# Last feed-forward, first half: activations and remainders in 512 columns, VectorE folds the pairs, ScalarE squares

## Chip, cores and metric

One Trainium2 chip, one NeuronCore. The metric is the device time in microseconds of one execution of the whole program; lower is better. All data are float32; matrix products run on values that are rounded to TensorE's fp32r format, with a correction for what the rounding drops.

## What is computed

The program is two model blocks one after the other on 256 tokens of width 1024 (`T = 256`, `DC = 8` chunks of 128 features). The change touches the last feed-forward of the second block alone:

```python
def sqrelu_mlp(h, w1, w2):
    return jnp.square(jax.nn.relu(h @ w1)) @ w2
...
        h_lat = h_lat + mod_l[5] * sqrelu_mlp(modulate(rmsnorm(h_lat, norm2_g[i]), mod_l[3], mod_l[4]),
                                              mlp_w1[i], mlp_w2[i])
    return rmsnorm(h_lat, final_g)
```

`h @ w1` widens 1024 features to 4096, which are `MC = 32` tiles of 128 features by 256 tokens; `@ w2` brings them back. Beside it run the dot products of the conditioning vector with `ada_w` (the `mod` values), of which eight tiles fall into this stage.

## The kernel before

**Split products.** A weight tile `w` is split into `whi = round(w)` (ScalarE, L930) and `wlo = w - whi` (VectorE, L1428); activations likewise into `xhi` and `xlo`. A product is the sum of three matmuls: `whi·xhi + whi·xlo + wlo·xhi`, each with 256 moving columns (one per token), into 256 columns of a PSUM bank.

**Units.** Weights stream from DRAM in units of 128 x 1024 floats (512 KB), 8 blocks of 128 x 128. In this stage (`mlp_up`, 32 units) one unit gives one output tile, so a unit is 8 blocks, 24 matmuls and one tile. The second half (`mlp_down`, 32 units) makes a tile of 4 units. It already uses the other form that `units` has (`both=m2`): rounded values and remainders lie in one buffer, a matmul of 512 columns takes `whi` against both at once, and one of 256 columns takes `wlo` against the rounded values, so a bank holds two partial results side by side.

**Rings.** There are four slots each for `raw` (as landed), `whi` and `wlo`, and four PSUM banks for tiles. SP issues the load of the next position when the slot four positions back is done with (`slots_done`, signalled by L1428 or by the dot product L1515, which takes a position of its own after every fourth unit).

**Order of work.** Every engine runs its own list of instructions strictly in the order in which the code emits it; semaphores are counters. In step j of the stage, for tile j:

- ScalarE: `hi()` rounds the weights of the unit three ahead (it waits for the load, and for TensorE to be done with unit j-1); then Relu from the PSUM bank into `mr` (L1382, waits `pe_units`, signals `tile_read`); then the rounding of tile j-1 of the squares, `mhi` (L1377, waits `y_f32`, signals `yhi_ready`).
- VectorE: the square `ms = mr*mr` (L2057, waits `tile_read`, signals `y_f32`); the remainder `mlo` of tile j-1 (`inner_lo`, L2052, waits `yhi_ready`); `lo()`, the weight remainder of the unit three ahead (L1428, signals `slots_done`, for which TensorE waits before that unit). After every fourth step comes `ada_dot` (L1515).
- TensorE: waits `slots_done` for its unit and `tile_read` for the bank, then 24 matmuls (L479, L480, L484; for the first two units L460 to L462, chunk by chunk as `xlo` appears).

The stage is a device loop of two passes of 16 steps on ScalarE and VectorE.

Of the kernel before, what the change touches and what calls it, by code (L numbers as in the profile page):

```python
# [18 lines left out]
F32R = mybir.dt.float32r  # L19
ALU = mybir.AluOpType  # L20
ACT = mybir.ActivationFunctionType
AX = mybir.AxisListType

P = 128
T = 256
D = 1024
DC = D // P
FF = 2816
FC = FF // P
# [6 lines left out]
MC = 4096 // P  # L36
# [18 lines left out]
          ("gla_r", 8), ("gla_out", DC), ("mlp_up", MC), ("mlp_down", MC)]  # L55
UNITS = sum(n for _, n in PHASES)
ADA_TILES = 6 * DC
PHASE_AT = {name: sum(n for _, n in PHASES[:i]) for i, (name, _) in enumerate(PHASES)}
assert PHASE_AT["up0"] % RING == 0 and LEAD == RING - 1

# [105 lines left out]
def at(t, k):  # L166

    return t[:, k * T:(k + 1) * T] if isinstance(k, int) else t[:, bass.ds(k * T, T)]
# [7 lines left out]
def program(nc, stream, xT, ctxT, vec, cst, rot, wa2, crow, out):  # L176
    ctx = ExitStack()

    def sb(name, cols, dt=F32, stack=ctx, rows=P):
        return stack.enter_context(nc.sbuf_tensor(name, [rows, cols], dt))  # L180

    with ctx:

        raw = sb("raw", RING * D)
        whi = sb("whi", RING * D, F32R)
# [17 lines left out]
        state = sb("state", 2 * GH * T)  # L203

        stage = ExitStack()
        xhi = sb("xhi", DC * T, F32R, stage)
        xlo = sb("xlo", DC * T, F32R, stage)
        stage.close()
        stage = ExitStack()
        csq_c = sb("csq_c", DC * T, F32, stage)  # L210
# [2 lines left out]
        stage = ExitStack()  # L213
# [7 lines left out]
        stage = ExitStack()  # L221
# [4 lines left out]
        stage = ExitStack()  # L226
# [3 lines left out]
        stage = ExitStack()  # L230
# [26 lines left out]
        stage = ExitStack()  # L257
# [7 lines left out]
        stage = ExitStack()  # L265
# [22 lines left out]
        stage = ExitStack()  # L288
        m2 = sb("m2", 2 * MC * T, F32R, stage)
        mhi, mlo = m2[:, 0:MC * T], m2[:, MC * T:2 * MC * T]  # L290
        mr = sb("mr", 4 * T, F32, stage)
# [10 lines left out]
        def ev(name):  # L302

            if name not in named:
                named[name] = ctx.enter_context(nc.semaphore(name))
            return named[name]
# [117 lines left out]
        def _(pe):  # L424
# [11 lines left out]
            def slot_of_next_unit():  # L436
# [6 lines left out]
                c.n["unit"] = u + 1  # L443
                return u % RING

            def units(n, K, hi, lo, sizes=(BLK,), lag=RING, chunks=None, then=None, after=0, final=None, both=None):

                blk, begin = 0, 0  # L450
                if chunks is not None and then is None:
                    pair = [slot_of_next_unit() for _ in range(2)]
                    for j in range(2):
                        tile_free(tile[0] + j, lag)
                    for k in range(K):
                        c.take(chunks)
                        for j, slot in enumerate(pair):
                            dst = ps[(tile[0] + j) % lag][:, 0:T]
                            w = slice(slot * D + k * P, slot * D + (k + 1) * P)
                            pe.matmul(dst, whi[:, w], at(hi, k), start=(k == 0), stop=False)  # L460
                            pe.matmul(dst, whi[:, w], at(lo, k), start=False, stop=False)
                            last = pe.matmul(dst, wlo[:, w], at(hi, k), start=False, stop=(k == K - 1))  # L462
                            if k == K - 1:
                                c.sig(last, pe_units)
                    blk, begin = 2 * K, 2
                for j in range(begin, n):
                    slot = slot_of_next_unit()
                    for b in range(sizes[j % len(sizes)]):
                        t, k = tile[0] + blk // K, blk % K
                        if k == 0:  # L470
                            tile_free(t, lag)
                        dst = ps[t % lag][:, 0:T]
                        w = slice(slot * D + b * P, slot * D + (b + 1) * P)
                        if chunks is not None and j == 0 and begin == 0:
                            c.take(chunks)
                        if final is not None and k >= K - LATE and (k == K - 1 or blk < K):
                            pe.wait_ge(y_ready, final - (K - 1 - k))
                        if both is None:
                            pe.matmul(dst, whi[:, w], at(hi, k), start=(k == 0), stop=False)  # L479
                            pe.matmul(dst, whi[:, w], at(lo, k), start=False, stop=False)  # L480
                        else:
                            halves = both[:, :].rearrange("p (s n) -> p s n", s=2)[:, :, k * T:(k + 1) * T]
                            pe.matmul(ps[t % lag][:, 0:2 * T], whi[:, w], halves, start=(k == 0), stop=False)  # L483
                        last = pe.matmul(dst, wlo[:, w], at(hi, k), start=False, stop=(k == K - 1))  # L484
                        blk += 1
                    c.sig(last, pe_units)
                    if then is not None and j == after:
                        then()
                tile[0] += blk // K
# [403 lines left out]
            column_stat_of([ssum[:, 0:T], at(sq, 1)])  # L893
            spread()
            keep_warm(14)
            units(MC, DC, xhi, xlo, chunks=x_ready)
            c.take(y_ready, MC - LATE)
            c.n["y_ready"] += LATE
            looped(DC // 2, 8, MC, mhi, mlo, lag=2, final=c.n["y_ready"], both=m2)
# [6 lines left out]
        def _(act):  # L906
            c = Counts(act)

            def settled():


                act.wait_ge(ev("tables"), 16)

            def hi(n=1):

                for _ in range(n):
                    u = c.n.get("hi_ready", 0)
                    if u >= UNITS:
                        return
                    s = u % RING  # L920
                    pos, step = c.position(u, c.per.get("hi_ready", 0))
                    r = pos % RING
                    assert step % RING == 0
                    landed = 16 * (pos // RING + 1)
                    if step:
                        landed = c.i * (16 * step // RING) + landed
                    act.wait_ge(raw_ready[r], landed)
                    if u >= RING:
                        act.wait_ge(pe_units, c.value(hi_ready, 1 - RING))
                    c.sig(act.activation(whi[:, s * D:(s + 1) * D], raw[:, r * D:(r + 1) * D], ACT.Copy), hi_ready)  # L930
# [439 lines left out]
            sqrt_columns(D)  # L1370
            modulated(xhi, 3 * DC)
            c.n["pe_units"] = UNITS - 2 * MC
            with c.loop(2, {hi_ready: 16, pe_units: 16, tile_read: 16, y_f32: 16, yhi_ready: 16}) as i:
                def inner_hi(j):
                    settled()
                    c.take(y_f32)
                    c.sig(act.activation(at(mhi, i * 16 + j), at(ms, j % 4), ACT.Copy), yhi_ready)  # L1377

                for j in range(16):
                    hi()  # L1380
                    c.take(pe_units)
                    c.sig(act.activation(at(mr, j % 4), ps[j % 4][:, 0:T], ACT.Relu), tile_read)  # L1382
                    if j % 4:
                        inner_hi(j - 1)
                    if j % 4 == 3:
                        inner_hi(j)

            def gained(k):
                act.activation(at(h, k), at(h, k), ACT.Copy, scale=col("g_fin2", k)).then_inc(ev("gained"), 1)
# [23 lines left out]
        def _(dve):  # L1413
# [3 lines left out]
            def lo(n=1):  # L1417

                for _ in range(n):
                    u = c.n.get("unit", 0)  # L1420
                    if u >= UNITS:
                        return
                    w = slice(u % RING * D, (u % RING + 1) * D)
                    pos = c.n.get("slots_done", 0)
                    assert ORDER[pos] == ("w", u)
                    r = slice(pos % RING * D, (pos % RING + 1) * D)
                    c.take(hi_ready)
                    c.sig(dve.tensor_tensor(wlo[:, w], raw[:, r], whi[:, w], ALU.subtract), slots_done)  # L1428
                    c.n["unit"] = u + 1
# [615 lines left out]
            resid(1, None, gate=2 * DC, ahead=1, last_square=True)  # L2045
            reciprocal_columns()
            modulated(h, DC, 3 * DC, xlo, factor=RSTD)
            with c.loop(2, {hi_ready: 16, "unit": 16, slots_done: 20, tile_read: 16, y_f32: 16, yhi_ready: 16,
                            y_ready: 16}) as i:
                def inner_lo(j):  # L2050
                    c.take(yhi_ready)
                    c.sig(dve.tensor_tensor(at(mlo, i * 16 + j), at(ms, j % 4), at(mhi, i * 16 + j), ALU.subtract),  # L2052
                          y_ready)

                for j in range(16):
                    c.take(tile_read)
                    c.sig(dve.tensor_tensor(at(ms, j % 4), at(mr, j % 4), at(mr, j % 4), ALU.mult), y_f32)  # L2057
                    if j % 4:
                        inner_lo(j - 1)
                    lo()  # L2060
                    if j % 4 == 3:
                        inner_lo(j)
                        ada_dot(5 * DC + j // 4, i * 4 + (5 * DC + j // 4))
            c.again(slots_done)
            mod_of(5 * DC, 6 * DC, 0, 0, None)
            c.n["pe_units"] += MC
            clear_sum()

            def mlp_down(first, last=False):
# [137 lines left out]
```

## Time and profile before

| | |
|---|---|
| median of 3 runs | 966.36 us (965.63 to 967.92) |
| profiled execution, own time | 969.07 us |
| its span, first to last instruction | 967.3 us |
| TensorE matmul busy | 946.5 us, 98% |
| VectorE busy | 790.5 us, 82% |
| ScalarE busy | 550.8 us, 57% |
| mean granted TensorE clock | 0.994 of full speed |
| the stage: first matmul of the third unit | 782.54 us |
| first matmul of `mlp_down` | 867.98 us |
| last matmul of `mlp_down` | 956.70 us |

Starts in the trace are counted from the span's start. The busy shares are averages over stages; what counts here is who waits for whom between 782 and 877 us. A matmul's duration in the trace overlaps that of the next, so TensorE's pace is read from the distance between starts.

### The profile page before, as it was taken

How to read it: one execution, taken by the hardware profiler on the slowest of the kernel's cores; microseconds unless marked ns; L12 is line 12 of the kernel's file. 1: busy time of each engine (PE TensorE's matmuls, PEld its weight loads, DVE VectorE, ACT ScalarE, POOL GpSimd, SP SyncE). 2: the span in 40 equal slices, each digit the busy share in tenths (PEclk: the TensorE clock that was granted, in tenths of full speed). 3: DMA queues.
4: the chain of work that ended last, by engine and by line, in shares of the span. 5: the costliest groups of instructions: out<-in, count | busy, mean ns of one | idle time of the engine just before them, and what ended most of it. 6: DMA issues, size and time to landing. Idle time of an engine off the chain costs nothing.

```text
span 967.3 us, 20407 instructions
## 1 busy us (share of the span) xinstructions
PE 946.5 (98%) x7152; PEld 908.1 (94%) x7152; DVE 790.5 (82%) x1300; ACT 550.8 (57%) x890; POOL 1.8 (0%) x8
## 2 busy tenths in 40 slices
PE   9999999999998998999999999999999999999996
PEld 8999999999998988999999999988899999998885
DVE  6988899998997879999998987855867877776553
ACT  7445666565544665666565555886533465564432
POOL 0000000000000000000000000000000000000000
PEclk9999999999999999999999999999999999999998
DMA  8776576557775445555557666563673347676551
GB/s 321 270 244 217 174 240 196 178 194 253 263 244 196 156 154 171 179 192 193 177 192 263 237 241 191 170 214 142 236 241 136 131 153 234 226 235 221 183 185 44
DMA packets 53446, 195.50 MB, mean 202 GB/s; under 512 B 5934, under 2 KB 6062, under 8 KB 53264
## 3 DMA queue, kind: packets, MB, share of 16 engines
q1 hardware_dynamic: 53248, 193.72, 59.8%
q10 hardware_dynamic: 144, 1.05, 0.3%
q8 instruction: 36, 0.59, 0.2%
q14 instruction: 18, 0.15, 0.0%
HBM read 193.69 MB, written 1.05 MB: 201 GB/s over the span
## 4 chain that ended last, share of the span: by engine, by line
PE 86%; DVE 8%; ACT 4%; issue 1%; DMA 0%; DVEq 0%; ACTq 0%; SPq 0%
PE ps L484 24%; PE ps L479 21%; PE ps L480 21%; PE ps L483 6%; DVE wlo L1428 3%; PE ps L512 2%; PE ps L514 2%; PE ps L513 2%; ACT whi L930 1%; PE ps L528 1%; PE ps L742 1%; PE ps L758 1%; DVE rstd L1455 1%; DMA h<-xT 0%; DVE raw L1515 0%
## 5 line engine op out<-in xcount | busy, mean ns | idle before, releaser
L1428 DVE TENSOR_TENSOR wlo<-raw,whi 128x1024 fp32r<-128x1024 f32 x303 | 367.1, 1221 | 70.4 <-ACT whi L930 69.4
L930 ACT ACTIVATE whi<-raw 128x1024 fp32r<-128x1024 f32 x303 | 317.2, 1053 | 95.6 <-DMA raw<-stream 47.0
L479 PE MATMUL ps<-xhi,whi 128*128 128x256 f32 x1280 | 362.5, 283 | 1.8 <-DVE xlo L1450 0.9
L480 PE MATMUL ps<-xlo,whi 128*128 128x256 f32 x1280 | 359.7, 281 | 0.0
L484 PE MATMUL ps<-xhi,wlo 128*128 128x256 f32 x1280 | 359.7, 281 | 0.0
L479 PEld LDWEIGHTS ps<-xhi,whi 128*128 128x128 f32 x1280 | 241.9, 189 | 3.3 <-DVE xlo L1450 1.1
L480 PEld LDWEIGHTS ps<-xlo,whi 128*128 128x128 f32 x1280 | 241.9, 189 | 0.7 <-issue 0.5
L484 PEld LDWEIGHTS ps<-xhi,wlo 128*128 128x128 f32 x1280 | 241.9, 189 | 0.0
L479 PE MATMUL ps<-yhi,whi 128*128 128x256 f32 x400 | 112.5, 281 | 1.0 <-DVE wlo L1428 1.0
L480 PE MATMUL ps<-ylo,whi 128*128 128x256 f32 x400 | 112.2, 281 | 0.0
L484 PE MATMUL ps<-yhi,wlo 128*128 128x256 f32 x400 | 112.2, 281 | 0.0
L976 ACT ACTIVATE cv<-U,vt 128x256 f32<-128x256 f32 x88 | 45.0, 511 | 87.9 <-DVE U L1568 87.9
L483 PE MATMUL ps<-m,whi 128*128 128x512 f32 x256 | 88.9, 392 | 0.0
L479 PEld LDWEIGHTS ps<-yhi,whi 128*128 128x128 f32 x400 | 75.5, 189 | 1.6 <-issue 1.6
L480 PEld LDWEIGHTS ps<-ylo,whi 128*128 128x128 f32 x400 | 75.5, 189 | 0.0
L484 PEld LDWEIGHTS ps<-yhi,wlo 128*128 128x128 f32 x400 | 75.5, 189 | 0.0
L484 PE MATMUL ps<-m,wlo 128*128 128x256 f32 x256 | 71.6, 279 | 0.0
L483 PEld LDWEIGHTS ps<-m,whi 128*128 128x128 f32 x256 | 48.1, 188 | 10.6
L484 PEld LDWEIGHTS ps<-m,wlo 128*128 128x128 f32 x256 | 48.0, 188 | 0.0
L1470 DVE SCALAR_TENSOR_TENSOR cv<-U,vt,cv 128x256 f32<-128x256 f32 x96 | 46.0, 479 | 0.5 <-ACT cv L1062 0.5
L1476 DVE SCALAR_TENSOR_TENSOR cv<-U,vt,cv 128x256 f32<-128x256 f32 x96 | 45.7, 476 | 0.1
L1568 DVE TENSOR_TENSOR U<-ps,rstd 128x256 f32<-128x256 f32 x88 | 37.2, 423 | 6.0 <-PE ps L484 4.7
(303 smaller groups left out, 1364.6 us busy)
## 6 DMA issues: line engine op xcount, KB each, us to landing
raw<-stream SPq DMA_DIRECT2D x343, 512.0 KB, 4.0
side<-stream SPq DMA_DIRECT2D x16, 512.0 KB, 4.7
h<-xT SPq DMA_DIRECT2D x2, 512.0 KB, 5.6
c<-ctxT ACTq DMA_DIRECT2D x1, 1024.0 KB, 6.2
ct<-cst SPq DMA_DIRECT2D x1, 962.5 KB, 9.6
rt_tab<-rot SPq DMA_DIRECT2D x1, 704.0 KB
cr<-crow SPq DMA_DIRECT2D x1, 512.0 KB, 6.9
state<-crow SPq DMA_DIRECT2D x1, 512.0 KB, 7.7
```

Source lines behind the costliest of these rows:

```text
L479: pe.matmul(dst, whi[:, w], at(hi, k), start=(k == 0), stop=False)
L480: pe.matmul(dst, whi[:, w], at(lo, k), start=False, stop=False)
L483: pe.matmul(ps[t % lag][:, 0:2 * T], whi[:, w], halves, start=(k == 0), stop=False)
L484: last = pe.matmul(dst, wlo[:, w], at(hi, k), start=False, stop=(k == K - 1))
L512: pe.matmul(dst, hi[:, tok], whi[:, w], start=first, stop=False)
L513: pe.matmul(dst, lo[:, tok], whi[:, w], start=False, stop=False)
L930: c.sig(act.activation(whi[:, s * D:(s + 1) * D], raw[:, r * D:(r + 1) * D], ACT.Copy), hi_ready)
L976: c.sig(act.activation(at(cv, j), U[:, j * (T + 2) + 2:(j + 1) * (T + 2)], ACT.Copy, scale=vt_col(i * 12 + (base + 3 * j + 2))), tap_ready)
L1428: c.sig(dve.tensor_tensor(wlo[:, w], raw[:, r], whi[:, w], ALU.subtract), slots_done)
L1470: c.sig(dve.scalar_tensor_tensor(out=at(cv, j), in0=U[:, o + 1:o + T + 1], scalar=w1, in1=at(cv, j), op0=ALU.mult, op1=ALU.add), seq_dve)
L1476: return dve.scalar_tensor_tensor(out=at(cv, j), in0=U[:, o:o + T], scalar=w0, in1=at(cv, j), op0=ALU.mult, op1=ALU.add)
L1568: c.sig(dve.tensor_tensor(U[:, j * (T + 2) + 2:(j + 1) * (T + 2)], result(1), rstd[:, :], ALU.mult), tile_read)
```

## The change

The activations and their remainders get one buffer `x2`, so that `units` can take `whi` against both in one matmul of 512 columns (32 times 8 blocks). The two halves of a bank then have to be added. VectorE does this with a `tensor_reduce` over pairs (element n and element n + 256) from PSUM into `mr`, which also frees the bank (`tile_read`). ScalarE no longer reads the bank: it applies Relu in place on `mr`, rounds tile j-1 as before, and now also squares tile j into `ms`. The device loop becomes 32 steps written out.

```diff
-        xhi = sb("xhi", DC * T, F32R, stage)
-        xlo = sb("xlo", DC * T, F32R, stage)
+        x2 = sb("x2", 2 * DC * T, F32R, stage)
+        xhi, xlo = x2[:, 0:DC * T], x2[:, DC * T:2 * DC * T]
...
+                            else:
+                                pe.matmul(ps[(tile[0] + j) % lag][:, :], whi[:, w], halves_of(both, k), start=(k == 0), stop=False)
...
-            units(MC, DC, xhi, xlo, chunks=x_ready)
+            units(MC, DC, xhi, xlo, chunks=x_ready, both=x2)
...
+            def inner_hi(j):
+                c.again(y_f32)
+                c.sig(act.activation(at(mhi, j), at(ms, j % 4), ACT.Copy), yhi_ready)
+
+            for j in range(MC):
+                hi()
+                c.take(tile_read)
+                act.activation(at(mr, j % 4), at(mr, j % 4), ACT.Relu).then_inc(ev("relus"), 1)
+                if j:
+                    inner_hi(j - 1)
+                if j >= 4:
+                    act.wait_ge(y_ready, BEFORE_MLP + j - 3)
+                act.wait_ge(ev("relus"), j + 1)
+                c.sig(act.activation(at(ms, j % 4), at(mr, j % 4), ACT.Square), y_f32)
+            inner_hi(MC - 1)
...
-                for j in range(16):
-                    c.take(tile_read)
-                    c.sig(dve.tensor_tensor(at(ms, j % 4), at(mr, j % 4), at(mr, j % 4), ALU.mult), y_f32)
-                    if j % 4:
-                        inner_lo(j - 1)
-                    lo()
-                    if j % 4 == 3:
-                        inner_lo(j)
-                        ada_dot(5 * DC + j // 4, i * 4 + (5 * DC + j // 4))
+            for j in range(MC):
+                c.take(pe_units)
+                if j >= 4:
+                    c.take(y_f32)
+                c.sig(dve.tensor_reduce(at(mr, j % 4), ps[j % 4][:, :].rearrange("p (s n) -> p n s", s=2), AX.X, ALU.add), tile_read)
+                if j:
+                    inner_lo(j - 1)
+                lo()
+                if j % 4 == 3:
+                    ada_dot(5 * DC + j // 4)
+            inner_lo(MC - 1)
```

How the rows stand on the two engines. VectorE before, one step inside the stage (third tile): square, remainder of the tile before (its wait is a row of its own, since the loop counts with registers), weight remainder.

```order
L2057 TENSOR_TENSOR ms<-mr 128x256 [waits tile_read]
L141 REGISTER_ALU
L2052 ISA [waits yhi_ready]
L2052 REGISTER_ALU
L2052 TENSOR_TENSOR m2<-ms,m2 128x256
L141 REGISTER_ALU
L1428 TENSOR_TENSOR wlo<-raw,whi 128x1024 [waits hi_ready]
```

VectorE in the changed kernel, the last step of a group of four and the start of the next:

```order
L2066 TENSOR_REDUCE mr<-ps3 128x256 [waits y_f32,pe_units]
L2060 TENSOR_TENSOR m2<-ms,m2 128x256 [waits yhi_ready]
L1436 TENSOR_TENSOR wlo<-raw,whi 128x1024 [waits hi_ready]
L1523 SCALAR_TENSOR_TENSOR raw,moda<-raw,cr 128x1024 [waits raw_ready3]
L2066 TENSOR_REDUCE mr<-ps0 128x256 [waits y_f32,pe_units]
```

The square is gone, the fold of the bank stands in its place and waits for TensorE itself; the remainder of the tile before stands directly behind it, as the square's did.

ScalarE before, from one Relu to the next:

```order
L1382 ACTIVATE mr<-ps2 128x256 [waits pe_units]
L141 REGISTER_ALU
L141 REGISTER_ALU [waits tables]
L1377 ISA [waits y_f32]
L1377 ACTIVATE m2<-ms 128x256
L930 ACTIVATE whi<-raw 128x1024 [waits pe_units,raw_ready1]
L141 REGISTER_ALU
L1382 ACTIVATE mr<-ps3 128x256 [waits pe_units]
```

ScalarE in the changed kernel, the same stretch:

```order
L1387 ACTIVATE mr<-mr 128x256 [waits tile_read]
L1382 ACTIVATE m2<-ms 128x256 [waits y_f32]
L1393 ACTIVATE ms<-mr 128x256 [waits relus,y_ready]
L937 ACTIVATE whi<-raw 128x1024 [waits pe_units,raw_ready2]
L1387 ACTIVATE mr<-mr 128x256 [waits tile_read]
```

The Relu now waits for VectorE's fold (`tile_read`) and no longer for TensorE, and the rounding of the tile before (`m2<-ms`) still stands behind the Relu.

## Rows read from the trace of the kernel before

**Rows 1.** The page's first line and its busy times, whole span.
```profile
span 967.3 us, 20407 instructions
PE 946.5 (98%) x7152; PEld 908.1 (94%) x7152; DVE 790.5 (82%) x1300; ACT 550.8 (57%) x890; POOL 1.8 (0%) x8
```

**Rows 2.** Stretches: busy us of each engine, PEclk, DMA share, GB/s.
```profile
782.30:867.60 85.30, 85.30 (x721) 85.30 (x720) 67.42 (x106) 52.67 (x92) 0.00 (x0) 1.00 0.71 227
871.00:956.00 85.00, 85.00 (x492) 74.79 (x491) 46.49 (x55) 34.36 (x42) 0.00 (x0) 1.00 0.52 167
```

**Rows 3.** Timeline of TensorE: start, duration, line; stage begin, change of form, end.
```profile
782.54 0.28 PE L479 MATMUL ps<-xhi,whi 128*128 128x256 f32 x1
782.66 0.28 PE L480 MATMUL ps<-xlo,whi 128*128 128x256 f32 x1
...
867.98 0.48 PE L483 MATMUL ps<-m,whi 128*128 128x512 f32 x1
...
956.47 0.39 PE L483 MATMUL ps<-m,whi 128*128 128x512 f32 x1
956.70 0.28 PE L484 MATMUL ps<-m,wlo 128*128 128x256 f32 x1
```

**Rows 4.** Groups by form, 782.3 to 871: count, busy us, mean ns, idle before, releaser.
```profile
L2057 DVE TENSOR_TENSOR ms<-mr 128x256 f32<-128x256 f32 x32 | 13.6, 424 | 17.4 <-ACT mr L1382 17.4
L1515 DVE SCALAR_TENSOR_TENSOR raw<-raw,cr 128x1024 f32<-128x1024 f32 x8 | 9.8, 1219 | 0.0
L930 ACT ACTIVATE whi<-raw 128x1024 fp32r<-128x1024 f32 x32 | 33.8, 1057 | 8.2 <-DMA raw<-stream 8.0
L1377 ACT ACTIVATE m<-ms 128x256 f32 x32 | 13.2, 411 | 2.3 <-DVE ms L2057 2.3
L1382 ACT ACTIVATE mr<-ps 128x256 f32<-128x256 f32 x32 | 12.3, 384 | 23.9 <-PE ps L484 22.8 <-PE ps L462 1.0
```

**Rows 5.** Timeline of VectorE, one step and the dot product behind the next.
```profile
797.39 0.42 DVE L2057 TENSOR_TENSOR ms<-mr 128x256 f32<-128x256 f32 x1 [0.76 <-ACT mr L1382]
797.92 0.43 DVE L2052 TENSOR_TENSOR m<-ms,m 128x256 f32 x1
798.26 1.22 DVE L1428 TENSOR_TENSOR wlo<-raw,whi 128x1024 fp32r<-128x1024 f32 x1
...
801.12 1.22 DVE L1428 TENSOR_TENSOR wlo<-raw,whi 128x1024 fp32r<-128x1024 f32 x1
802.25 0.42 DVE L2052 TENSOR_TENSOR m<-ms,m 128x256 f32 x1
```

**Rows 6.** Timeline of ScalarE, the first tile and one step inside.
```profile
782.38 0.39 ACT L1382 ACTIVATE mr<-ps 128x256 f32<-128x256 f32 x1 [1.04 <-PE ps L462]
...
796.98 0.39 ACT L1382 ACTIVATE mr<-ps 128x256 f32<-128x256 f32 x1 [0.52 <-PE ps L484]
797.26 0.41 ACT L1377 ACTIVATE m<-ms 128x256 f32 x1
797.57 1.05 ACT L930 ACTIVATE whi<-raw 128x1024 fp32r<-128x1024 f32 x1
```

**Rows 7.** Groups by form, whole span: VectorE's reduces and a 512-column read of PSUM.
```profile
L1810 DVE TENSOR_REDUCE mx<-ps 128x1 f32<-128x256 f32 x8 | 3.3, 415 | 0.0
L1994 DVE TENSOR_TENSOR att<-ps,ct 128x512 f32<-128x512 f32 x4 | 2.7, 681 | 0.0
L1809 DVE TENSOR_REDUCE mx<-ps 128x1 f32<-128x128 f32 x8 | 2.3, 287 | 3.7 <-PE ps L629 3.7
```

**Rows 8.** Chain that ended last: a hand-over VectorE, ScalarE, VectorE without registers.
```profile
752.68 0.43 DVE rsil L2014
753.14 0.43 ACT zhi L1340
753.59 0.77 DVE zlo L2020 x2
```

**Rows 9.** Timeline of VectorE, from the last dot product into `mlp_down`.
```profile
870.94 1.22 DVE L1515 SCALAR_TENSOR_TENSOR raw<-raw,cr 128x1024 f32<-128x1024 f32 x1
872.08 0.08 DVE L1515 DVE_READ_ACCUMULATOR raw<-raw,cr  x1
...
873.24 2.36 DVE L1428 TENSOR_TENSOR wlo<-raw,whi 128x1024 fp32r<-128x1024 f32 x2 [0.22 <-DVE ssum L1464]
```

**Rows 10.** DMA issues, 776 to 868: count, KB each, median us from issue to landing.
```profile
raw<-stream SPq DMA_DIRECT2D x37, 512.0 KB, 4.3
```

More of the change, by code:

```diff
@@ L57 @@
 ADA_TILES = 6 * DC
+BEFORE_MLP = DC + 2 * FC + DC
 PHASE_AT = {name: sum(n for _, n in PHASES[:i]) for i, (name, _) in enumerate(PHASES)}
@@ L444, in slot_of_next_unit, with halves_of @@
                 return u % RING
+            def halves_of(both, k):
+                return both[:, :].rearrange("p (s n) -> p s n", s=2)[:, :, k * T:(k + 1) * T]
             def units(n, K, hi, lo, sizes=(BLK,), lag=RING, chunks=None, then=None, after=0, final=None, both=None):
@@ L459, in units @@
                             w = slice(slot * D + k * P, slot * D + (k + 1) * P)
-                            pe.matmul(dst, whi[:, w], at(hi, k), start=(k == 0), stop=False)
-                            pe.matmul(dst, whi[:, w], at(lo, k), start=False, stop=False)
+                            if both is None:
+                                pe.matmul(dst, whi[:, w], at(hi, k), start=(k == 0), stop=False)
+                                pe.matmul(dst, whi[:, w], at(lo, k), start=False, stop=False)
+                            else:
+                                pe.matmul(ps[(tile[0] + j) % lag][:, :], whi[:, w], halves_of(both, k), start=(k == 0), stop=False)
                             last = pe.matmul(dst, wlo[:, w], at(hi, k), start=False, stop=(k == K - 1))
@@ L481, in units @@
                         else:
-                            halves = both[:, :].rearrange("p (s n) -> p s n", s=2)[:, :, k * T:(k + 1) * T]
-                            pe.matmul(ps[t % lag][:, 0:2 * T], whi[:, w], halves, start=(k == 0), stop=False)
+                            pe.matmul(ps[t % lag][:, :], whi[:, w], halves_of(both, k), start=(k == 0), stop=False)
                         last = pe.matmul(dst, wlo[:, w], at(hi, k), start=False, stop=(k == K - 1))
@@ L1372, in _ @@
             c.n["pe_units"] = UNITS - 2 * MC
[L1373 to L1377, printed above, removed]
-                for j in range(16):
-                    hi()
-                    c.take(pe_units)
-                    c.sig(act.activation(at(mr, j % 4), ps[j % 4][:, 0:T], ACT.Relu), tile_read)
-                    if j % 4:
-                        inner_hi(j - 1)
-                    if j % 4 == 3:
-                        inner_hi(j)
+            def inner_hi(j):
[12 more added lines that the diff above has]
+            inner_hi(MC - 1)
             def gained(k):
@@ L2047, in _, with inner_lo @@
             modulated(h, DC, 3 * DC, xlo, factor=RSTD)
[L2048 to L2055, printed above, removed]
-                    c.take(tile_read)
-                    c.sig(dve.tensor_tensor(at(ms, j % 4), at(mr, j % 4), at(mr, j % 4), ALU.mult), y_f32)
-                    if j % 4:
-                        inner_lo(j - 1)
-                    lo()
-                    if j % 4 == 3:
-                        inner_lo(j)
-                        ada_dot(5 * DC + j // 4, i * 4 + (5 * DC + j // 4))
+            assert c.n["y_ready"] == BEFORE_MLP
+            def inner_lo(j):
+                c.take(yhi_ready)
+                c.sig(dve.tensor_tensor(at(mlo, j), at(ms, j % 4), at(mhi, j), ALU.subtract), y_ready)
+            for j in range(MC):
[9 more added lines that the diff above has]
+            inner_lo(MC - 1)
             c.again(slots_done)
             mod_of(5 * DC, 6 * DC, 0, 0, None)
-            c.n["pe_units"] += MC
             clear_sum()
```

## Prediction, on record before the changed kernel ran

> **What bounds the kernel now.** I read the page first: TensorE is busy for 98% of the span and VectorE for 82% [rows 1]. An average hides what a stage can spare, so I went on to two stretches: in the stage that changes TensorE is never idle (85.30 of 85.30 us), VectorE is busy for 67 of them and ScalarE for 53, at full clock; in `mlp_down` TensorE is never idle either [rows 2]. So before, TensorE sets the pace of both. Its pace comes from starts. From 782.54 to 867.98 it does 30 units (720 matmuls), 85.44 us, so 118.7 ns a matmul, 0.356 us a block, 2.848 us a unit. In `mlp_down`, 256 blocks in 512 + 256 columns end with the matmul at 956.70; with 0.12 us for it that is 88.84 us, 0.347 us a block, 2.776 us a unit [rows 3].
>
> Then who waits behind it: VectorE's square waits 17.4 us in all for the Relu, which itself waits 22.8 us for TensorE; ScalarE waits 8.0 us for loads [rows 4]. None of this reaches TensorE. The reader should see that VectorE's slack is one wait, for the Relu, 0.76 us in a step [rows 5], and that it is some 17 us in 32 steps.
>
> **The change part by part.**
>
> *TensorE.* Three matmuls of 256 columns (0.356 us) become one of 512 and one of 256 (0.347 us): 0.0093 us saved, times 256 blocks, 2.4 us, if nothing else sets the pace. That is all it can bring; columns stay 768 a block, only one start of three is saved.
> The Trainium skill says something else of 512 columns: "TensorE: Matmul & The Clock Gate", section Back-to-back issue gap, gives a sustained spacing of about 131 ns a matmul at 512 columns in a stream of weight loads and matmuls. The trace does not agree: from the 512-column matmul at 956.47 to the next start it is 0.23 us [rows 3]. By the Trainium skill's figure a block would cost 0.1 us less, an estimate of 25 us less for 256 blocks; the sum goes by the row.
>
> *VectorE, durations.* The square goes: it holds the engine 0.34 us until the next can start (remainder to weight remainder, 797.92 to 798.26, is the same shape of operation). The fold comes. This shape has no row. A reduce of 128 elements takes 287 ns and one of 256 takes 415 [rows 7], that is 128 ns for 128 elements; 512 elements read give 287 + 384 = 671 ns, and a two-operand pass over 512 PSUM columns takes 681. I take 0.68 us. Low end: it pays for the 256 results alone, 0.42 us. High end: pairs 256 columns apart cost twice, as a pass over 1024, 1.22 us [rows 4]. The other work of a step stays: 0.34 us for the remainder, 1.14 us from one start to the next for `wlo` or the dot product (801.12 to 802.25 is 1.13, the dot's with its read-out at 872.08 is 1.14) [rows 5, 9]; with the fold's own start to start of some 0.61 that is 2.09 a step and 1.15 more for the dot, 9.5 us in a group of four. TensorE needs 4 x 2.776 = 11.1. By busy time alone VectorE fits.
>
> *VectorE, order.* It doesn't fit by order. Before, square j needs Relu j, and the remainder of tile j-1 needs its rounding, which ScalarE does behind Relu j, beside the square; one wait covers both. Now Relu j waits for the fold of tile j, the rounding of tile j-1 stands behind that Relu in ScalarE's list, and VectorE's next instruction after the fold is the remainder that needs this rounding. VectorE so stands idle for a round trip in every step. Its length: fold 0.68; hand-over to ScalarE 0.03 (752.68 + 0.43 to 753.14); Relu until the rounding may start 0.31 (797.26 to 797.57, same kind and shape from SBUF); rounding 0.41; hand-over back 0.02 (753.57 to 753.59) [rows 6, 8]. The remainder starts 1.45 us after the fold, `wlo` 0.34 later, the next fold 1.14 later: **2.93 us a step**, and a group of four with its dot product takes 4 x 2.93 + 1.15 = **12.87 us** against 11.10 for TensorE now and 11.39 before. Behind the waiting remainder are queued `wlo` (TensorE waits for that through `slots_done`), the dot product and so SP's next load.
>
> *Can ScalarE or the loads lengthen it?* In a step ScalarE does Relu, rounding and square, 0.31 each from start to start, and `hi` 1.05 [rows 4, 6]: 2.0 of 2.93, and 0.9 us to spare before the next Relu. A raw slot freed at the end of step j-2 is wanted by `hi` two steps later, behind the square: 2 x 2.93 + 1.7 - 3.0, about 4.5 us at the tightest; landing takes 4.3 us [rows 10], and the spare 0.9 covers the rest. I put nothing on the path for it.
>
> *The walk.* The first fold starts where the first Relu did, 782.4 [rows 6]. Step 0 has no remainder, so fold 1 is at 782.4 + 0.61 + 1.14 = 784.15. Fold 4 is at +3 x 2.93 + 1.15 = 794.1, fold 28 six groups later at 871.3, fold 31 at 880.1. TensorE lives for a while on the weights prepared ahead: unit j+3 may start 1.79 + 1.22 = 3.0 us after fold j, and at 2.776 us a unit from 782.54 it catches up with that at about unit 14; from there VectorE feeds it. At the end: `wlo` of the last step is done at 883.1 and the dot begins at 883.0. From the dot to the first `wlo` of `mlp_down` it was 870.94 to 873.24, 2.30 us [rows 9], and is 0.34 more now, since the last remainder stands there: start 885.65, done 886.9. That is the weights of the fourth unit of `mlp_down` (the first three got theirs inside the stage), which TensorE starts at 886.9. Before it was 867.98 + 3 x 2.776 = 876.3. From there on nothing differs: TensorE is the pace again [rows 2], and it has no idle time in which to catch up. So **+10.5 us**.
>
> *Costed at nothing:* the loop written out and its register work (they sat in VectorE's wait of 0.76, which is gone, and the walk uses hand-overs without registers); the square on ScalarE (inside the 2.0 us; if `hi` were late by more than 0.9, it would add 0.31 a step); the buffer `x2` (same bytes); the first two units, chunk by chunk (paced by `xlo` first and the end moves by under 0.1 us).
>
> **Sum.** Profiled execution: span 967.3 + 10.5 = 977.8, its own time 969.07 + 10.5 = 979.6. The median of the runs shown is 966.36, 2.7 under that execution's own time; on the median the forecast is **976.9 us**.
>
> **The rivals.**
>
> *A, the round trip as costed*, 976.9, say 973.5 to 981.5 for hand-overs off by 0.1 us a step either way (3 us in 30 steps) and some late loads. Chance 0.70.
>
> *B, the fold is cheap.* At 0.42 us a step is 2.67, a group 11.83, still over 11.39. Fold 31 comes 30 x 0.26 = 7.8 us earlier: +2.6 us, 969.0. For it: nothing but that only 256 values are written. Against it: the reduces of before cost by what they read, with one value written [rows 7]. Chance 0.08.
>
> *C, the fold is dear.* 1.22 us: 0.54 more in 31 steps, 17 us on top, 993.6. No row has pairs that far apart. Chance 0.09, most of it for lesser surcharges, around 985.
>
> *D, VectorE keeps up* and TensorE's 2.4 us come through: 964.0. It needs a group under 11.1 us, a step under 2.49; the round trip would have to shrink by 0.44 us, more than the Relu's share. From 11.39 a group on down it is faster than before, that is a step under 2.56. For it speaks the busy sum of 9.5 us; against it the order. The change would then do what the matmul count says. Chance 0.05. By the 131 ns of the Trainium skill's page ("TensorE: Matmul & The Clock Gate", Back-to-back issue gap) D would bring about 25 us more, an estimate that the 0.23 us of [rows 3] speaks against.
>
> *E, loads join in.* If `hi` comes late by 0.4 us beyond its 0.9 in half of the steps, 6 us more, 983. For it: ScalarE already waits for loads 8.0 us in this stage. Against it: slower consumption leaves the queues emptier. Chance 0.08.
>
> **How the numbers follow.** A measurement of this kernel tells no less than about 0.2%, 1.9 us, from no change. Low end of the range: B's 969.0, which leaves D and a sliver out. High end: 985, for E and the milder half of C. That leaves 0.05 + 0.04 below and some 0.06 above, so the range holds a little over 8 in 10. Faster by over 0.2% is D nearly whole, 0.05; within 0.2% the seam between B and D, 0.04; slower 0.91.
>
> **What would show it.** In the profile after: folds near 0.68 us; VectorE idle before the remainder for some 0.85 us in every step, released by ScalarE's rounding, about 26 us in all; steps of 2.93 and groups of 12.9 us on VectorE; TensorE without gaps until about unit 14 (some 820 us), then waiting for `wlo`, 10 to 11 us in all up to the fourth unit of `mlp_down`; first 512-column matmul of `mlp_down` near 877 and 8 x 0.347 a unit within units; the rest shifted by 10.5. The prediction is wrong if the fold's duration is far from 0.68, if the rounding turns out done when the remainder is reached, or if ScalarE's Relu is held by `hi` and not by the fold.

## The result

| | changed | before | ratio, 95% interval |
|---|---|---|---|
| first comparison, medians of 6 | 982.29 us | 967.03 us | 1.017, 1.0155 to 1.0185 |
| second, on another occasion (4 and 17 runs) | 980.09 us | 967.42 us | 1.0135, 1.0112 to 1.0158 |

The change makes the kernel slower, by 15.3 us in the first comparison and 12.7 us in the second. The forecast was 976.9, 10.5 us slower, with a range from 969 to 985. The profiled execution is one of the two longest of its six: these took 986.73 and 986.76 us, the other four 981.04 to 982.37. That matters below.

The page's first lines, to set beside [rows 1]:

```profile
span 984.9 us, 19695 instructions
PE 953.3 (97%) x6896; PEld 898.0 (91%) x6896; DVE 797.6 (81%) x1300; ACT 559.6 (57%) x922; POOL 1.8 (0%) x8
```

256 matmuls are gone (7152 to 6896), the span is 17.6 us longer, and no engine's share shows why. The groups by form in the stage do (782.3 to 890, columns as in [rows 4]):

```profile
L490 PE MATMUL ps<-x,whi 128*128 128x512 f32 x240 | 87.1, 403 | 7.0 <-DVE wlo L1436 7.0
L490 PEld LDWEIGHTS ps<-x,whi 128*128 128x128 f32 x240 | 45.0, 188 | 22.3 <-DVE wlo L1436 13.3
...
L937 ACT ACTIVATE whi<-raw 128x1024 fp32r<-128x1024 f32 x34 | 35.6, 1046 | 3.7 <-PE ps L491 2.6 <-DMA raw<-stream 1.1
L2066 DVE TENSOR_REDUCE mr<-ps 128x256 f32<-128x512 f32 x32 | 21.9, 685 | 1.3 <-PE ps L470 1.3
L2060 DVE TENSOR_TENSOR m<-ms,m 128x256 fp32r<-128x256 f32 x32 | 13.6, 426 | 24.5 <-ACT m L1382 24.5
L1387 ACT ACTIVATE mr<-mr 128x256 f32<-128x256 f32 x32 | 13.4, 418 | 37.6 <-DVE mr L2066 37.6
L1393 ACT ACTIVATE ms<-mr 128x256 f32<-128x256 f32 x32 | 12.9, 402 | 0.0
```

VectorE waits 24.5 us in 31 steps for ScalarE's rounding, which waits behind a Relu that waits for VectorE's fold; and TensorE, which before was never idle here [rows 2], now waits for VectorE's `wlo`, in its matmuls (first row) and in the weight loads ahead of them (second row). One step of VectorE's timeline, to set beside [rows 5]:

```profile
800.95 1.22 DVE L1436 TENSOR_TENSOR wlo<-raw,whi 128x1024 fp32r<-128x1024 f32 x1
802.09 0.68 DVE L2066 TENSOR_REDUCE mr<-ps 128x256 f32<-128x512 f32 x1
803.56 0.43 DVE L2060 TENSOR_TENSOR m<-ms,m 128x256 fp32r<-128x256 f32 x1 [0.79 <-ACT m L1382]
803.91 1.22 DVE L1436 TENSOR_TENSOR wlo<-raw,whi 128x1024 fp32r<-128x1024 f32 x1
805.04 0.68 DVE L2066 TENSOR_REDUCE mr<-ps 128x256 f32<-128x512 f32 x1
```

and what ScalarE does between that fold and that remainder:

```profile
802.81 0.42 ACT L1387 ACTIVATE mr<-mr 128x256 f32<-128x256 f32 x1 [0.97 <-DVE mr L2066]
803.13 0.40 ACT L1382 ACTIVATE m<-ms 128x256 fp32r<-128x256 f32 x1
803.44 0.40 ACT L1393 ACTIVATE ms<-mr 128x256 f32<-128x256 f32 x1
803.75 1.04 ACT L937 ACTIVATE whi<-raw 128x1024 fp32r<-128x1024 f32 x1
```

From fold to fold it is 2.95 us; the fold ends at 802.77, Relu starts at 802.81, the rounding ends at 803.53, the remainder starts at 803.56. A group of four steps with its dot product is 12.96 us (folds at 796.18 and 809.14), against TensorE's 11.1.

TensorE's starts give the split of the 17.6 us. The third unit of `mlp_up` starts at 784.58, `mlp_down` at 883.01, its last matmul at 974.43 (before: 782.54, 867.98, 956.70, [rows 3]):

- 2.04 us lie ahead of the stage. They are not the change's: in the second profile of the same kernel this start is at 781.72, in profiles of other kernels of this study between 778 and 782. Part of that distance is a fall of the granted clock at 308 us, which the profile of before and the first one of after both have and no other profile has (see the last section).
- **13.0 us in the stage**, 98.43 against 85.44. In the second profile it is 98.40.
- 2.7 us in `mlp_down`, 91.42 against 88.72. In the second profile it is 88.82, so nothing.
- The end after it is 0.1 us shorter.

The 2.7 us are the clock. Stretches of the profile after (columns as in [rows 2]) and TensorE's timeline at the seam, where `mlp_up` ends and `mlp_down` begins:

```profile
875.00:880.00 5.00, 3.94 (x22) 3.04 (x20) 3.80 (x6) 3.62 (x8) 0.00 (x0) 1.00 0.78 248
880.00:885.00 5.00, 2.06 (x7) 1.71 (x7) 3.42 (x6) 3.43 (x9) 0.00 (x0) 0.71 0.55 179
885.00:890.00 5.00, 5.00 (x21) 4.30 (x20) 4.24 (x8) 2.00 (x2) 0.00 (x0) 0.61 0.64 228
890.00:895.00 5.00, 5.00 (x31) 4.42 (x30) 2.22 (x2) 1.75 (x2) 0.00 (x0) 1.00 0.69 229
```

```profile
879.79 0.28 PE L491 MATMUL ps<-x,wlo 128*128 128x256 f32 x1
883.01 0.79 PE L490 MATMUL ps<-m,whi 128*128 128x512 f32 x1 [2.94 <-DVE wlo L1436]
883.60 0.41 PE L491 MATMUL ps<-m,wlo 128*128 128x256 f32 x1
883.81 0.63 PE L490 MATMUL ps<-m,whi 128*128 128x512 f32 x1
884.24 0.41 PE L491 MATMUL ps<-m,wlo 128*128 128x256 f32 x1
```

TensorE was idle 2.94 us before `mlp_down`; then a block takes 0.64 us where 0.347 is usual, for nine blocks. The granted clock is at its half level (1.2 GHz), and back at 2.4 by 889. The second profile has the same idle time and the clock did not fall:

```profile
880.12 0.50 PE L490 MATMUL ps<-m,whi 128*128 128x512 f32 x1 [2.95 <-DVE wlo L1436]
880.45 0.28 PE L491 MATMUL ps<-m,wlo 128*128 128x256 f32 x1
880.57 0.39 PE L490 MATMUL ps<-m,whi 128*128 128x512 f32 x1
```

So the change costs 13 us in the stage in both profiled executions, and 2.7 us more in one of them.

### The profile page after: what moved, and what is told of

Read it like the earlier page. It is cut to its first block, busy times and chain, and to the rows that moved or that the text cites. A ratio compares the mean times of both kernels' runs of the same rounds, so it can differ in the third digit from the quotient of the medians.

```text
span 984.9 us, 19695 instructions
## 1 busy us (share of the span) xinstructions
PE 953.3 (97%) x6896; PEld 898.0 (91%) x6896; DVE 797.6 (81%) x1300; ACT 559.6 (57%) x922; POOL 1.8 (0%) x8
## 3 DMA queue, kind: packets, MB, share of 16 engines
q10 hardware_dynamic: 144, 1.05, 0.3%
HBM read 193.69 MB, written 1.05 MB: 198 GB/s over the span
## 4 chain that ended last, share of the span: by engine, by line
PE 77%; DVE 14%; ACT 6%; issue 2%; DMA 1%; DVEq 0%; SPq 0%; ACTq 0%
PE ps L491 20%; PE ps L487 18%; PE ps L488 17%; DVE wlo L1436 6%; PE ps L490 6%; DVE mr L2066 2%; PE ps L519 2%; PE ps L521 2%; PE ps L520 2%; ACT mr L1387 1%; DVE raw L1523 1%; ACT whi L937 1%; ACT ms L1393 1%; PE ps L535 1%; PE ps L749 1%
## 5 line engine op out<-in xcount | busy, mean ns | idle before, releaser
L491 PE MATMUL ps<-x,wlo 128*128 128x256 f32 x1280 | 360.1, 281 | 0.0
L487 PE MATMUL ps<-x,whi 128*128 128x256 f32 x1040 | 295.8, 284 | 3.1 <-DVE wlo L1436 1.7
L488 PE MATMUL ps<-x,whi 128*128 128x256 f32 x1040 | 293.0, 282 | 0.0
L491 PEld LDWEIGHTS ps<-x,wlo 128*128 128x128 f32 x1280 | 242.6, 190 | 0.0
L487 PEld LDWEIGHTS ps<-x,whi 128*128 128x128 f32 x1040 | 197.5, 190 | 4.8 <-DVE wlo L1436 2.6
L488 PEld LDWEIGHTS ps<-x,whi 128*128 128x128 f32 x1040 | 197.5, 190 | 0.7 <-issue 0.5
L490 PE MATMUL ps<-m,whi 128*128 128x512 f32 x256 | 91.5, 400 | 2.9 <-DVE wlo L1436 2.9
L490 PE MATMUL ps<-x,whi 128*128 128x512 f32 x240 | 87.1, 403 | 7.0 <-DVE wlo L1436 7.0
L490 PEld LDWEIGHTS ps<-x,whi 128*128 128x128 f32 x240 | 45.0, 188 | 22.3 <-DVE wlo L1436 13.3
L1478 DVE SCALAR_TENSOR_TENSOR cv<-U,vt,cv 128x256 f32<-128x256 f32 x96 | 45.9, 478 | 0.5 <-ACT cv L1069 0.5
```

The lines of the kernel that those rows point to most:

```text
L490: pe.matmul(ps[t % lag][:, :], whi[:, w], halves_of(both, k), start=(k == 0), stop=False)
L1478: c.sig(dve.scalar_tensor_tensor(out=at(cv, j), in0=U[:, o + 1:o + T + 1], scalar=w1, in1=at(cv, j), op0=ALU.mult, op1=ALU.add), seq_dve)
```

## The experiments

**1. VectorE: weight remainder ahead of activation remainder.** If the round trip is the cost, something independent under it should take it away.

```diff
                 c.sig(dve.tensor_reduce(at(mr, j % 4), ...), tile_read)
-                if j:
-                    inner_lo(j - 1)
                 lo()
+                if j:
+                    inner_lo(j - 1)
                 if j % 4 == 3:
                     ada_dot(5 * DC + j // 4)
```

> The changed kernel with one edit on VectorE: in each step the weight remainder wlo stands ahead of the activation remainder, so that the round trip fold, Relu, rounding runs beside wlo (1.14 us). Theory 1 (the round trip is what costs): VectorE no longer waits 0.79 us a step, a group of four needs 4 x 2.09 + 1.15 = 9.5 us against TensorE's 11.1, TensorE sets the pace again and its 2.4 us come through: about 964.6 against 967.0 before. Theory 2 (the fold itself, its reads of PSUM beside TensorE's writes, or the 512-column form costs): waits stay somewhere and the time stays over 975.

Measured: 964.68 us against 966.71, ratio 0.9974 (0.9963 to 0.9984). The theory of the round trip holds, to 0.1 us of its number. VectorE's timeline in this kernel:

```profile
806.40 0.69 DVE L2066 TENSOR_REDUCE mr<-ps 128x256 f32<-128x512 f32 x1 [0.61 <-PE ps L491]
807.01 1.22 DVE L1436 TENSOR_TENSOR wlo<-raw,whi 128x1024 fp32r<-128x1024 f32 x1
808.14 0.42 DVE L2060 TENSOR_TENSOR m<-ms,m 128x256 fp32r<-128x256 f32 x1
809.17 0.69 DVE L2066 TENSOR_REDUCE mr<-ps 128x256 f32<-128x512 f32 x1 [0.61 <-PE ps L491]
```

The fold, as long as before, now waits for TensorE, and the remainder for nobody. A step is 2.77 us, TensorE's. The stage takes 83.20 us (781.24 to 864.44): 240 blocks of 0.347 us.

**2. ScalarE: rounding of tile j-1 ahead of Relu j.** The same round trip cut at its other end, with VectorE's list untouched.

```diff
                 hi()
+                if j:
+                    inner_hi(j - 1)
                 c.take(tile_read)
                 act.activation(at(mr, j % 4), at(mr, j % 4), ACT.Relu).then_inc(ev("relus"), 1)
-                if j:
-                    inner_hi(j - 1)
```

> The changed kernel with one edit on ScalarE: the rounding of tile j-1 stands ahead of Relu j instead of behind it; VectorE's list is untouched. Theory 1: the remainder finds its rounding done, VectorE never waits there, same time as with wlo ahead, about 964.6. Theory 2 (it is VectorE's load, not the order between the two lists): still over 975. If only one of the two edits helps, the account of the round trip is incomplete.

Measured: 964.31 us, ratio 0.9972 (0.9961 to 0.9984). The same gain, the same stage of 83.20 us. Either edit is enough, so it is the order between the two lists and not the work on either. ScalarE's timeline shows the rounding under way before the fold is done:

```profile
803.25 0.40 ACT L1382 ACTIVATE m<-ms 128x256 fp32r<-128x256 f32 x1
804.24 0.42 ACT L1389 ACTIVATE mr<-mr 128x256 f32<-128x256 f32 x1 [0.59 <-DVE mr L2066]
```

**3. A shorter fold.** The sum is left out: VectorE copies the first 256 columns, so the product with the activations' remainders is missing.

```diff
-                c.sig(dve.tensor_reduce(at(mr, j % 4), ps[j % 4][:, :].rearrange("p (s n) -> p n s", s=2), AX.X, ALU.add), tile_read)
+                c.sig(dve.tensor_copy(at(mr, j % 4), ps[j % 4][:, 0:T]), tile_read)
```

> The changed kernel with the fold replaced by a copy of the first 256 columns of the bank; the second half (the product of the weights with the activations' remainders) is left out of the sum. All waits stay. Copy of 256 columns 0.42 us against 0.685. Theory 1 (fold lies on VectorE's path once a step): a step is 2.955 - 0.265 = 2.69, group 11.9, 8 us less than the changed kernel: about 974. Theory 2 (waits and hand-overs only, fold covered): no change, 982.

Measured: 973.73 us, ratio 1.0059 (1.0037 to 1.008). The stage takes 90.85 us against 98.4, 7.6 us less where 8 us were expected, so the fold lies on VectorE's path once a step. That the median also meets the expected 974 is partly luck: it is 6.4 us under the changed kernel's second median and 8.6 under its first, and a fall of the clock is in the profiled execution. The wait behind it is the same 0.79 us:

```profile
806.63 0.42 DVE L2066 COPY mr<-ps 128x256 f32<-128x256 f32 x1
807.85 0.43 DVE L2060 TENSOR_TENSOR m<-ms,m 128x256 fp32r<-128x256 f32 x1 [0.79 <-ACT m L1382]
808.19 1.22 DVE L1436 TENSOR_TENSOR wlo<-raw,whi 128x1024 fp32r<-128x1024 f32 x1
809.32 0.42 DVE L2066 COPY mr<-ps 128x256 f32<-128x256 f32 x1
```

A step is 2.69 us. In this profile too TensorE stood idle (2.42 us) at the seam, and the clock fell: `mlp_down` takes 90.10 us and not 88.7. The shortest of the four executions, 970.85 us, has the highest mean granted clock (0.998 against 0.995 and 0.996).

**4. Exact waits at the start of `mlp_down`.** The profile after had shown a wait of which the forecast knew nothing: the first unit of `mlp_down` started at 883.01, although its own `wlo`, of the step before, was done at 879.93. In TensorE's loop the awaited count is worked out from the position 8 units on; since the last dot product's position lies in between, it asks for one slot more than the first three units need. VectorE's weight remainders of the profile after, that unit's own and the one which it waited for:

```profile
878.71 1.22 DVE L1436 TENSOR_TENSOR wlo<-raw,whi 128x1024 fp32r<-128x1024 f32 x1
881.66 1.22 DVE L1436 TENSOR_TENSOR wlo<-raw,whi 128x1024 fp32r<-128x1024 f32 x1
```

```diff
-            looped(DC // 2, 8, MC, mhi, mlo, lag=2, final=c.n["y_ready"], both=m2)
+            units(8, MC, mhi, mlo, lag=2, final=c.n["y_ready"], both=m2)
+            looped(DC // 2 - 1, 8, MC, mhi, mlo, lag=2, both=m2)
```

> The changed kernel with the first 8 units of mlp_down taken out of TensorE's loop, so that they wait for exactly their own weights; inside the loop the wait counts one slot more than needed for the first three units, because the position of the last dot product falls between them. Theory 1 (that wait costs once VectorE is late): the first unit of mlp_down starts 2.95 us earlier and TensorE's gap before it goes from 2.94 us to under 1.5; net about 1.5 us less, and with the gap the drop of the granted clock goes too, 2.6 us more in those executions that had it: 978 to 981. Theory 2 (the clock drop comes from the 0.4 us gaps of the whole stage): gap shorter, drop stays, 980 to 982.

Measured: 979.12 us, ratio 1.0118 (1.0099 to 1.0137). TensorE's waits at the seam:

```profile
876.98 0.47 PE L490 MATMUL ps<-m,whi 128*128 128x512 f32 x1 [0.60 <-DVE mr L2067]
...
886.22 0.50 PE L490 MATMUL ps<-m,whi 128*128 128x512 f32 x1 [0.67 <-DVE wlo L1437]
```

One idle stretch of 2.95 us has become two short ones. The first unit starts 96.10 us after the third unit of `mlp_up`, 2.3 us earlier than in the second profile of the changed kernel (98.40) and not the 2.95 us that were expected: with its weights there, it still waits for a fold to free its bank (`mr L2067`). The clock stayed at its full level in the one profile and no run is over 979.4. The two stages together take 185.75 us against 187.22 in the second profile of the changed kernel: 1.5 us, as expected for this run. (The two profiles are from different chips.) The medians differ by 1.0 us from the changed kernel's second comparison and by 3.2 from its first, too uneven to size the clock's part.

**5. The changed kernel again, and with the gap filled.** The first is for comparison on the same chip; its profile is used above.

> The changed kernel as it is, on the chip of the two kernels beside it, for comparison: 981 to 987, median near 982.

```diff
             c.take(y_ready, MC - LATE)
             c.n["y_ready"] += LATE
+            for _ in range(22):
+                pe.matmul(ps[5][:, 0:T], xhi[:, 0:P], xhi[:, 0:T], start=True, stop=True)
             looped(DC // 2, 8, MC, mhi, mlo, lag=2, final=c.n["y_ready"], both=m2)
```

> The changed kernel with 22 more matmuls of 256 columns, of no use, between the last unit of mlp_up and the first of mlp_down (22 x 0.119 = 2.6 us into a bank that nobody reads); they fill the 2.94 us in which TensorE waited for weights. Nothing that is waited for changes. Theory 1 (the granted clock falls because TensorE stands idle there, and the first matmuls of mlp_down run at half clock): clock stays at full level, mlp_down's first blocks take 0.347 us and not 0.64, up to 2.6 us less than the changed kernel in its own runs beside it. Theory 2 (the fall comes from elsewhere, such as the short gaps before): the fall stays and the time is the same.

Measured: 980.09 us for the changed kernel, 980.80 with the gap filled (ratios 1.0135 and 1.0131). No difference, and this does not decide between the theories: the profile of the changed kernel beside it had no fall of the clock to take away. The filling did what it was to do, idle time fell from 2.95 to 0.31 us:

```profile
877.06 2.79 PE L907 MATMUL ps<-x 128*128 128x256 f32 x22
880.16 0.49 PE L490 MATMUL ps<-m,whi 128*128 128x512 f32 x1 [0.31 <-DVE wlo L1438]
```

**6. The kernel before, its loops written out.** A control for the part of the change that the forecast costed at nothing (the edit is the loop's form alone: 32 steps in place of two passes of 16, on ScalarE and VectorE).

```diff
-            with c.loop(2, {hi_ready: 16, pe_units: 16, tile_read: 16, y_f32: 16, yhi_ready: 16}) as i:
...
+            for j in range(MC):
```

> The kernel before with only its device loops of this stage on ScalarE and VectorE written out as 32 steps, as in the changed kernel. Theory 1 (the loop's form costs nothing on either side): within 0.1% of before, 967. Theory 2 (part of the changed kernel's loss, such as its 2 us ahead of the stage in the profiled execution, comes with the longer program): 1 to 2 us over before.

> The kernel before with its loops of the stage written out, again: the first time it was 0.9986 of before, interval 0.9972 to 1.0. Theory 1 (no cost, no gain of the loop's form): interval holds 1. Theory 2: again about 0.15% under before, 1 to 1.5 us.

Measured: 0.9986 (0.9972 to 1.0) the first time, 1.0011 (0.9998 to 1.0024) the second. The two lie on either side of 1, so no effect that these runs can tell. The stage takes 85.43 us in the second profile, as before, but 84.48 us in the first, at full granted clock and with no wait of TensorE:

```profile
778.50 0.28 PE L479 MATMUL ps<-xhi,whi 128*128 128x256 f32 x1
862.98 0.39 PE L483 MATMUL ps<-m,whi 128*128 128x512 f32 x1
```

That is 0.352 us for a block of three matmuls in all 30 units, where the other two profiles of this form have 0.356. Why one kernel shows both was not looked into; it makes the price of the old form, and with it the gain of the new one, uncertain by 1 us.

**7. The repaired order again, alone and with exact waits.**

> Same kernel as the first of the study (wlo ahead of the remainder), now beside the kernel before written out, to tell what the 512-column form brings by itself. Theory 1 (TensorE's 0.0093 us a block): 2.4 us under the written-out kernel before and under before. Theory 2 (half of the gain is the loop that is gone): only about 1 us under the written-out one.

> wlo ahead of the remainder and the first 8 units of mlp_down outside TensorE's loop, so with exact waits. Theory 1 (the wait for one slot more costs only when VectorE is late): same as wlo ahead alone, within 0.1%. Theory 2 (it always costs a little): 0.5 to 1.5 us less.

Measured, beside before at 967.78: wlo ahead 965.50 us, 0.9981 (0.9968 to 0.9993); with exact waits as well 964.53 us, 0.9968 (0.9954 to 0.9983); the written-out kernel before of experiment 6 beside them 969.18. The 512-column form is worth 2.2 us in the traces against the stage of 85.44 and 85.43 us (83.20 us in each of the four profiles that have it without a starved TensorE), 1.3 us against the one of 84.48, and 2.0 and 2.3 us in the two comparisons with before. Against the written-out kernel it is 3.7 us, more than the 2.4 that were expected; the written-out kernel's own median was 1.4 us over before on this occasion and 1.8 under on the other, and what moves it was not settled. The exact waits change nothing that can be told where TensorE isn't starved: the median is 1.0 us lower, which by itself would suit either expectation, but the intervals overlap, and the stages in the trace are equal (83.20 and 88.62 against 83.20 and 88.63).

## Why the prediction was right, and where it was short

- **The main step held.** The forecast put the cost into a round trip between two lists, not into VectorE's load, with a remainder 1.45 us behind the fold and a step of 2.93 us. The trace has 1.47 and 2.95, the wait 0.79 us and 24.5 us in all where some 26 were forecast. Experiments 1 and 2 remove it from either side and all of the loss goes with it.
- **The fold.** 0.68 us from the reduces of [rows 7], 0.685 measured. Rivals B and C (cheap, dear) are out; pairs 256 columns apart cost no more than neighbours' reads. Experiment 3 shows the term on the path.
- **TensorE's gain.** 2.4 us forecast for 256 blocks. The 240 blocks after the first two units gave 2.24 us (85.44 - 83.20) once VectorE kept up; 240 x 0.0093 is 2.23. The rows behind the forecast give 0.0090 a block (0.3560 - 0.3470), so 2.3 us for 256; and against the stage of 84.48 us the gain is 1.3. Rival D was right in its price and wrong in its condition. A block stayed at 0.347 us, so the 131 ns a matmul at 512 columns of the Trainium skill ("TensorE: Matmul & The Clock Gate", Back-to-back issue gap) do not fit this stream.
- **Loads, rival E,** stayed out: ScalarE waited 1.1 us for one.
- **Where TensorE starves.** I had it catch up with VectorE at about unit 14. It waits from 799.27 on, the eighth unit: I had counted units from the wrong one at 782.54, which is the start of the third; and even by that count the walk's own numbers give about unit 19, not 14. Neither entered the sum. The sign "10 to 11 us in all" of waiting looks met, 7.0 us in the stage and 2.94 ahead of `mlp_down`, but it named the wrong quantity: 10.5 is the distance to before. Against TensorE's new pace the walk implies some 12.8 us up to the fourth unit of `mlp_down`, and the starts show about 15 in the stage alone (98.43 - 83.20). The idle time of the profile is less, because a matmul's duration reaches past the start of the next (0.39 us for one of 512 columns, 0.23 from start to start).
- **The step that was short** is the end of the walk, "the weights of the fourth unit of `mlp_down` ..., which TensorE starts at 886.9". It took each of the first three units to wait for its own weights. In the loop's form of the wait they wait for one slot more. The first unit so starts 2.95 us later than its weights allow, and the fourth follows at TensorE's pace, behind three whole units, instead of right behind its `wlo`. That makes 13.0 us where 10.5 were forecast. Experiment 4 sizes the parts: the form of the wait is 1.5 us; of the remaining 1.0, some 0.66 are steps 0.02 us longer than forecast and 0.3 lie between the last fold and the fourth unit's `wlo`. That wait stood in the code that the change does not touch; before, it cost nothing, since TensorE was never ahead.
- **The clock** was not in the sum at all. It adds 2.7 us in the first profile and nothing in the second. At the seam a long idle stretch comes ahead of each fall, in two profiles (2.94 and 2.42 us), and a stretch as long without a fall in one. What decides it was not settled, nor how many of the unprofiled runs had one. The two executions at 987 us have a mean granted clock of 0.991, the four at 981 to 982 one of 0.993 to 0.996, which fits a fall in the two; but they differ by more than 4 us, and a fall at the seam accounts for 2.7.
- **In the range partly by luck.** The upper half of the range was there for late loads and a dear fold. Neither came. Of the 5.4 us between the forecast and the first median the traces put 2.5 to the loop's wait and the longer steps, which are in every profile of the changed kernel; the rest is not in every execution, and the second median (12.7 us over before) lacks it. The range was made for neither.

## What to carry to other kernels

When an operation moves from one engine to another, write both engines' lists side by side and look for an instruction that waits for something queued behind what it has itself just released: busy shares said that VectorE fits (9.5 of 11.1 us), the order made it 12.96. The repair cost nothing here: put independent work of the right length (here 1.14 us of work, where the wait was 0.8) between the two, in either list. And where a change takes an engine off the lead, reread the waits that were free as long as it led; a conservative count then has a price.

## What the runs showed of the hardware

- A reduce over pairs that lie 256 columns apart in PSUM, 512 values read and 256 written, takes 0.685 us on VectorE; the line through the two reduces to one value of [rows 7] gives 0.671.
- The same idle stretch of TensorE, 2.94 and 2.95 us at the same place of the same program, was followed by nine blocks at half clock in one execution and by none in another.
- Shorter waits came ahead of a fall too. In the profile of before TensorE waits 1.05 us (until 303.23) and 1.24 us (until 307.30), and the granted clock is at its half level from about 308 to 311; the first profile of after has the same at that place. The other ten profiles have waits of about 1 and 1.2 us there and no fall. Before's rows (columns as in [rows 2]):

```profile
307.30 0.39 PE L479 MATMUL ps<-ohi,whi 128*128 128x256 f32 x1 [1.24 <-DVE olo L1726]
308.00:312.00 4.00, 4.00 (x23) 4.00 (x22) 0.74 (x2) 1.06 (x1) 0.00 (x0) 0.58 0.44 133
```

- A block of three matmuls of 256 columns has two paces at full granted clock, each held over many units: 0.356 us (before, 190 to 235 us and in the stage) and 0.352 us (before, 240 to 300 us; the first profile of experiment 6 in the stage). No run shows what sets it.
- With no registers in the waits, handing over between VectorE and ScalarE took 0.03 to 0.04 us each way.
